# Branch ends of a two-block network: a new order for the two tiles' norms, turns and splits

## The reference, cut to what matters

```python
for layer in range(4):
    g = norm_g[layer]
    h = h + 0.5 * rmsnorm(swiglu(rmsnorm(h, g[0]), ffn_w_in[layer, 0], ffn_w_out[layer, 0]), g[1])
    u = rmsnorm(h, g[2])
    m = mixer(u)          # swa, gla, rwkv7, swa
    h = h + rmsnorm(m, g[3])
    h = h + 0.5 * rmsnorm(swiglu(rmsnorm(h, g[4]), ffn_w_in[layer, 1], ffn_w_out[layer, 1]), g[5])
```

## Time and profile before

| | |
|---|---|
| Median of 3 runs | 3441.63 us (3441.36 to 3445.28) |
| Span of the profiled execution (its own time) | 3441.5 us |
| Instructions in the profile | 49232 |
| TensorE busy | 3274.3 us |
| VectorE busy | 1961.2 us |
| ScalarE busy | 1516.9 us |
| Mean granted TensorE clock | 0.980 |

### The profile page before, as it was taken

The page is one execution under the profiler, slowest core; times in us unless marked ns, Lnnn a source line. Parts: engine busy times, 40 slices in busy tenths (PEclk is TensorE's granted clock), DMA queues, the critical chain, the costliest instruction groups (busy, mean ns, idle before and its releaser), DMA issues.

```text
span 3441.5 us, 49232 instructions
## 1 busy us (share of the span) xinstructions
PE 3274.3 (95%) x21142; PEld 2885.6 (84%) x21142; DVE 1961.2 (57%) x2964; ACT 1516.9 (44%) x2538; POOL 177.4 (5%) x201
## 2 busy tenths in 40 slices
PE   6998999989999999998999999999999999999898
PEld 6987998978898997686989987987878887887797
DVE  4556555557555555674555566555446555825777
ACT  3445444454444443213444454444544434524554
POOL 0000000003000000140000000001001000100100
PEclk9999999999999999998999999999999999999999
DMA  6563656555556544414556554551013333531452
GB/s 225 184 201 105 208 184 210 188 177 178 190 184 210 189 154 154 142 44 137 187 191 208 184 176 153 184 179 28 26 62 110 110 121 136 173 97 62 134 185 98
DMA packets 411238, 521.99 MB, mean 152 GB/s; under 512 B 41575, under 2 KB 353500, under 8 KB 410892
## 3 DMA queue, kind: packets, MB, share of 16 engines
q1 hardware_dynamic: 405980, 516.23, 45.7%
q0 software_dynamic: 816, 2.10, 0.2%
q10 hardware_dynamic: 4224, 0.52, 0.1%
HBM read 516.19 MB, written 2.10 MB: 151 GB/s over the span
## 4 chain that ended last, share of the span: by engine, by line
PE 87%; DVE 7%; ACT 4%; issue 1%; DMA 1%; POOL 0%; SPq 0%; DVEq 0%; ACTq 0%; POOLq 0%
PE ps L186 24%; PE ps L187 24%; PE ps L188 23%; PE ps L178 5%; PE ps L196 3%; PE ps L1226 2%; PE ps L559 1%; PE ps L1938 1%; PE ps L3802 1%; PE ps L3799 1%; DVE small L1283 1%; ACT a L1246 1%; DVE a L716 0%; PE ps L3478 0%; DVE xt L699 0%
## 5 line engine op out<-in xcount | busy, mean ns | idle before, releaser
L186 PE MATMUL ps<-a 128*128 128x256 f32 (+1 forms) x4832 | 1528.4, 316 | 35.5 <-DVE a L716 13.9
L188 PE MATMUL ps<-a 128*128 128x256 f32 (+1 forms) x4664 | 1466.6, 314 | 0.0
L187 PE MATMUL ps<-a 128*128 128x256 f32 (+1 forms) x4536 | 1432.1, 316 | 0.0
L186 PEld LDWEIGHTS ps<-a 128*128 128x128 f32 x4832 | 929.7, 192 | 101.5 <-DVE a L716 13.9
L188 PEld LDWEIGHTS ps<-a 128*128 128x128 f32 x4664 | 897.7, 192 | 52.8
L187 PEld LDWEIGHTS ps<-a 128*128 128x128 f32 x4536 | 873.4, 193 | 50.6
L892 DVE TENSOR_TENSOR a<-ring,a 128x1024 fp32r<-128x1024 f32 x594 | 693.6, 1221 | 350.3 <-ACT a L886 350.3
L886 ACT ACTIVATE a<-ring 128x1024 fp32r<-128x1024 f32 x594 | 585.7, 1047 | 234.6 <-PE ps L188 233.7
L990 ACT ACTIVATE tmp<-ps 128x256 f32<-128x256 f32 x176 | 67.6, 384 | 508.6 <-PE ps L188 508.6
L996 DVE TENSOR_TENSOR a<-tmp,ps 128x256 f32<-128x256 f32 x176 | 74.1, 421 | 300.9 <-ACT tmp L990 300.9
L617 POOL TENSOR_TENSOR small<-small,cst 128x1 f32<-128x1 f32 (+1 forms) x78 | 58.3, 749 | 2806.2 <-DVE small L612 1965.7
(11 more groups left out here) (379 smaller groups left out, 3862.1 us busy)
## 6 DMA issues: line engine op xcount, KB each, us to landing
ring<-in_ffn_w_in_dram SPq DMA_DIRECT2D x220, 1024.0 KB, 7.4
ring<-in_ffn_w_out_dram SPq DMA_DIRECT2D x121, 1024.0 KB, 5.0
ring<-in_ada_w_dram SPq DMA_DIRECT2D x48, 1024.0 KB, 5.4
ring<-in_swa_w_qkv_dram SPq DMA_DIRECT2D x12, 1024.0 KB, 7.9
ring<-in_gla_w_in_dram SPq DMA_DIRECT2D x12, 1024.0 KB, 6.8
ring<-in_rwkv_w_rkv_dram SPq DMA_DIRECT2D x12, 1024.0 KB, 5.1
ring<-in_na_w_qkv_dram SPq DMA_DIRECT2D x12, 1024.0 KB, 5.2
ring<-in_swa_w_o_dram SPq DMA_DIRECT2D x8, 1024.0 KB, 5.7
```

The lines of the kernel that those rows point to most:

```text
L186: pe.x.matmul(out, lh, rh, start=start and i == 0, stop=False)
L187: pe.x.matmul(out, lh, rl, start=False, stop=False)
L188: ins = pe.x.matmul(out, ll, rh, start=False, stop=stop and i == n - 1)
```

## The change

`act_finish`, `dve_finish` and `pe_finish`, which served both kinds of end through flags, are replaced by one function for each kind and engine.

In a feed-forward end VectorE adds tile 0 into h before it splits the opened weights, not after; takes the mean of tile 1 between the two halves of tile 0's gain; scales tile 1 before it splits tile 0; and does both ada pairs at the end. ScalarE squares h of tile 1 before the first ada copy and scales tile 1 before the second. TensorE does the second pair's products into bank 6 instead of bank 3, behind a wait for tile 1's gain product.

In a mixer end TensorE transposes tile 0 inside tile 1's projection, ahead of its last two quarters (the last `k0` step, or `q == 2` of the second half). VectorE takes tile 0's gain between the two scales of tile 1, and its two splits around tile 1's add; the ada pair comes last. ScalarE splits tile 0 before it squares h of tile 1, and copies the ada row after that.

SP's list is the same, and GpSimd's four powers come in the same order.

```diff
--- before.py
+++ after.py
@@ -282,11 +282,14 @@
             load_block(K, sp, (tag, "wo", i, k0), w, k0, 4, i * 512, 512, (K.s.pe, (tag, "wo", tiles[-1], i, k0)))
 
 
-def pe_out(K, pe, tag, x, tiles, first):
+def pe_out(K, pe, tag, x, tiles, first, amid=None):
+
     for t in tiles:
         for i in range(2):
             bank = K.ps[:, 2 * (t + first) + i, :]
             for k0 in (0, 4):
+                if amid is not None and (t, i, k0) == (tiles[-1], 1, 4):
+                    amid()
                 c = K.w[tag, "wo", i, k0]
                 pe.wait_ge(*c.landed)
                 wv = v3(c.buf, 512)
@@ -425,13 +428,16 @@
     sp_splitB(K, sp, S, 0, w, 0, D, lambda i, k0: (K.s.pe, (tag, "wo", tiles[-1], i, k0)))
 
 
-def pe_split_out(K, pe, S, tag, xs, tiles, first, halves=(0, 1)):
+def pe_split_out(K, pe, S, tag, xs, tiles, first, halves=(0, 1), amid=None):
+
     s, (xh, xl) = K.s, xs
     for t in tiles:
         pe.wait_ge(*s.dve.at(tag, "turned", t, 1))
         for i in halves:
             bank = K.ps[:, 2 * (t + first) + i, :]
             for q in range(4):
+                if amid is not None and (t, i, q) == (tiles[-1], 1, 2):
+                    amid()
                 c, raw, wh, wl = S.of(K, 4 * i + q, 512)
                 pe.wait_ge(*s.dve.at("lo", S.tag, 4 * i + q))
                 ins = mm3(pe, bank, [((xh[:, 2 * q + k, tk(t)], xl[:, 2 * q + k, tk(t)]), (wh[:, k, :], wl[:, k, :])) for k in range(2)],
@@ -691,9 +697,9 @@
               ).then_inc(*s.pe.up(tag, t, "turn", half))
 
 
-def dve_gain(K, dve, tag, t, gcol):
+def dve_gain(K, dve, tag, t, gcol, halves=(0, 1)):
     s = K.s
-    for half in range(2):
+    for half in halves:
         f = slice(4 * half, 4 * half + 4)
         dve.wait_ge(*s.pe.at(tag, t, "turn", half))
         dve.x.tensor_tensor(K.xt3(T)[:, f, tk(t)], v3(K.ps[:, 2 * t + half, :], 128), bc(gcol[:, f], 2, [128, 4, 128]),
@@ -708,9 +714,9 @@
         act.x.activation(xh[:, k, tk(t)], K.xt3(T)[:, k, tk(t)], AF.Copy).then_inc(*s.act.up("xh", f, t, half))
 
 
-def dve_split_x(K, dve, f, t):
+def dve_split_x(K, dve, f, t, halves=(0, 1)):
     (xh, xl), s = K.xs[f], K.s
-    for half in range(2):
+    for half in halves:
         k = slice(4 * half, 4 * half + 4)
         dve.wait_ge(*s.act.at("xh", f, t, half))
         dve.x.tensor_tensor(xl[:, k, tk(t)], K.xt3(T)[:, k, tk(t)], xh[:, k, tk(t)].bitcast(F32), SUB).then_inc(
@@ -721,95 +727,113 @@
     return [K.s.dve.at(tag, t, "xt", half) for half in range(2)]
 
 
-def act_finish(K, act, tag, src, ready, nxt, f=None, early=False, pairs=0):
-
+def act_ffn_end(K, act, tag, src, ready, f):
 
     act_square(K, act, tag, 0, src[0], ready[0])
-    if nxt:
-        act_square_h(K, act, tag, 0)
-        if early:
-            act_norm(K, act, tag, 0)
+    act_square_h(K, act, tag, 0)
     act_square(K, act, tag, 1, src[1], ready[1])
-    if nxt and not early:
-        act_norm(K, act, tag, 0)
-    if pairs:
-        act_ada(K, act, 2, 2)
-    if nxt:
-        act_square_h(K, act, tag, 1)
-        if f is not None:
-            act_split_x(K, act, f, 0, xt_ready(K, tag, 0))
-    if pairs == 2:
-        act_ada(K, act, 2, 2)
-    if nxt:
-        act_norm(K, act, tag, 1)
+    act_norm(K, act, tag, 0)
+    act_square_h(K, act, tag, 1)
+    act_ada(K, act, 2, 2)
+    if f is not None:
+        act_split_x(K, act, f, 0, xt_ready(K, tag, 0))
+    act_norm(K, act, tag, 1)
+    act_ada(K, act, 2, 2)
     if f is not None:
         act_split_x(K, act, f, 1, xt_ready(K, tag, 1))
 
 
-def dve_finish(K, dve, tag, src, coef, gcol, f=None, early=False, pairs=0, bias=None, opened=None):
-
-    row, nxt = K.rows[tag, "g"], gcol is not None
+def dve_ffn_end(K, dve, tag, src, gcol, f, opened):
+
+    row = K.rows[tag, "g"]
     for half in range(2):
-        dve_scale(K, dve, tag, 0, half, src[0], row, coef, bias)
-    if opened is not None:
-        dve_open(K, dve, opened, 1)
+        dve_scale(K, dve, tag, 0, half, src[0], row, 0.5)
     dve_add(K, dve, tag, 0)
-    if nxt:
-        dve_mean_h(K, dve, tag, 0)
-        if early:
-            dve_norm(K, dve, tag, 0)
-    dve_scale(K, dve, tag, 1, 0, src[1], row, coef, bias)
-    if nxt and not early:
-        dve_norm(K, dve, tag, 0)
-    dve_scale(K, dve, tag, 1, 1, src[1], row, coef, bias)
+    dve_open(K, dve, opened, 1)
+    dve_mean_h(K, dve, tag, 0)
+    dve_scale(K, dve, tag, 1, 0, src[1], row, 0.5)
+    dve_norm(K, dve, tag, 0)
+    dve_scale(K, dve, tag, 1, 1, src[1], row, 0.5)
     dve_add(K, dve, tag, 1)
-    if nxt:
-        dve_gain(K, dve, tag, 0, gcol)
-    if pairs:
-        dve_ada(K, dve, 2)
-    if nxt:
-        dve_mean_h(K, dve, tag, 1)
-        if f is not None:
-            dve_split_x(K, dve, f, 0)
-        dve_norm(K, dve, tag, 1)
-        dve_gain(K, dve, tag, 1, gcol)
+    dve_gain(K, dve, tag, 0, gcol, (0,))
+    dve_mean_h(K, dve, tag, 1)
+    dve_gain(K, dve, tag, 0, gcol, (1,))
+    dve_norm(K, dve, tag, 1)
+    if f is not None:
+        dve_split_x(K, dve, f, 0)
+    dve_gain(K, dve, tag, 1, gcol)
     if f is not None:
         dve_split_x(K, dve, f, 1)
-    if pairs == 2:
+    for _ in range(2):
         dve_ada(K, dve, 2)
 
 
+def act_mixer_finish(K, act, tag, src, ready, f):
+
+    act_square(K, act, tag, 0, src[0], ready[0])
+    act_square_h(K, act, tag, 0)
+    act_norm(K, act, tag, 0)
+    act_square(K, act, tag, 1, src[1], ready[1])
+    act_split_x(K, act, f, 0, xt_ready(K, tag, 0))
+    act_square_h(K, act, tag, 1)
+    act_ada(K, act, 2, 2)
+    act_norm(K, act, tag, 1)
+    act_split_x(K, act, f, 1, xt_ready(K, tag, 1))
+
+
+def dve_mixer_finish(K, dve, tag, src, gcol, f, bias):
+
+    row = K.rows[tag, "g"]
+    for half in range(2):
+        dve_scale(K, dve, tag, 0, half, src[0], row, 1.0, bias)
+    dve_add(K, dve, tag, 0)
+    dve_mean_h(K, dve, tag, 0)
+    dve_norm(K, dve, tag, 0)
+    dve_scale(K, dve, tag, 1, 0, src[1], row, 1.0, bias)
+    dve_gain(K, dve, tag, 0, gcol)
+    dve_scale(K, dve, tag, 1, 1, src[1], row, 1.0, bias)
+    dve_split_x(K, dve, f, 0, (0,))
+    dve_add(K, dve, tag, 1)
+    dve_split_x(K, dve, f, 0, (1,))
+    dve_mean_h(K, dve, tag, 1)
+    dve_norm(K, dve, tag, 1)
+    dve_gain(K, dve, tag, 1, gcol)
+    dve_split_x(K, dve, f, 1)
+    dve_ada(K, dve, 2)
+
+
 def pool_finish(K, pool, tag, nxt):
-    pool_rsqrt(K, pool, (tag, 0, "y"), K.sm[tag, 0][:, 2:3])
-    if nxt:
-        pool_rsqrt(K, pool, (tag, 0, "h"), K.sm[tag, 0][:, 5:6])
-    pool_rsqrt(K, pool, (tag, 1, "y"), K.sm[tag, 1][:, 2:3])
-    if nxt:
-        pool_rsqrt(K, pool, (tag, 1, "h"), K.sm[tag, 1][:, 5:6])
-
-
-def pe_finish(K, pe, tag, nxt, pairs=0):
-
+    for t in range(2):
+        pool_rsqrt(K, pool, (tag, t, "y"), K.sm[tag, t][:, 2:3])
+        if nxt:
+            pool_rsqrt(K, pool, (tag, t, "h"), K.sm[tag, t][:, 5:6])
+
+
+def pe_ffn_end(K, pe, tag):
 
     s = K.s
-    if pairs:
-        K.free.clear()
-        rows, sums = Turns(K, (2, 3)), Turns(K, (4, 5))
-        pe_ada_products(K, pe, rows)
-    if nxt:
-        pe_turn_norm(K, pe, tag, 0)
-    if pairs:
-        if pairs == 2:
-            m = pe.ada
-            pe.ada += 2
-            pe_ada_products(K, pe, rows)
-            pe.ada = m
-        pe.wait_ge(*s.dve.at(tag, 0, "g1"))
-        pe_ada_turns(K, pe, sums, 2)
-    if nxt:
-        pe_turn_norm(K, pe, tag, 1)
-    if pairs == 2:
-        pe_ada_turns(K, pe, sums, 2)
+    K.free.clear()
+    rows, sums = Turns(K, (2, 6)), Turns(K, (4, 5))
+    pe_ada_products(K, pe, rows)
+    pe_turn_norm(K, pe, tag, 0)
+    m = pe.ada
+    pe.ada += 2
+    pe.wait_ge(*s.dve.at(tag, 1, "g1"))
+    pe_ada_products(K, pe, rows)
+    pe.ada = m
+    pe.wait_ge(*s.dve.at(tag, 0, "g1"))
+    pe_ada_turns(K, pe, sums, 2)
+    pe_turn_norm(K, pe, tag, 1)
+    pe_ada_turns(K, pe, sums, 2)
+
+
+def pe_mixer_finish(K, pe, tag):
+
+    K.free.clear()
+    pe_ada_products(K, pe, Turns(K, (2, 3)))
+    pe.wait_ge(*K.s.dve.at(tag, 0, "g1"))
+    pe_ada_turns(K, pe, Turns(K, (4, 5)), 2)
+    pe_turn_norm(K, pe, tag, 1)
 
 
 
@@ -1031,7 +1055,7 @@
         if f == 0:
             pe_first(K, pe)
     pe_core(K, pe, f)
-    pe_finish(K, pe, ("f", f), K.ffn[f].gcol is not None, 2)
+    pe_ffn_end(K, pe, ("f", f))
     K.s.pe.seal("end", ("f", f))
 
 
@@ -1045,7 +1069,7 @@
             act_split_x(K, act, f, t, xt_ready(K, K.ffn[f].normed, t))
     act_core(K, act, f, act_silu)
     act_open(K, act, f)
-    act_finish(K, act, ("f", f), down_banks(K), down_halves(K, f), K.ffn[f].gcol is not None, K.ffn[f].next, False, 2)
+    act_ffn_end(K, act, ("f", f), down_banks(K), down_halves(K, f), K.ffn[f].next)
     K.s.act.seal("end", ("f", f))
 
 
@@ -1082,7 +1106,7 @@
             dve_split_x(K, dve, f, t)
     dve_core(K, dve, f, dve_gate)
     dve_open(K, dve, f, 0)
-    dve_finish(K, dve, ("f", f), down_banks(K), 0.5, K.ffn[f].gcol, K.ffn[f].next, False, 2, None, f)
+    dve_ffn_end(K, dve, ("f", f), down_banks(K), K.ffn[f].gcol, K.ffn[f].next, f)
```

(16 more changed lines are left out.)

## The result

The changed kernel takes 3429.72 us (median of 4 runs, 3428.72 to 3430.52); the kernel before took 3443.45 us on the same chip (4 runs, 3441.36 to 3445.46). The ratio is 0.9958, with a 95% interval from 0.9944 to 0.9972: about 14 us, or 0.4%, faster. The profiled run took 3430.12 us, with a span of 3428.1 us.

What follows compares the result with a forecast made beforehand. TensorE, busy 95% of the span, bounds the kernel; only its gaps and half clock can be won. 3441.5 - 11.5 (feed-forward ends) + 0.6 (mixer ends) - 3.0 (clock) = 3427.6, stated as 3427.5 us, range 3420 to 3436.5.

Steps and rivals of the forecast that it cites:

- step 1: Feed-forward end, VectorE: tile 0's add no longer waits for the opened weights' split, so it starts about 0.96 us earlier.
- step 2: Feed-forward end, VectorE: tile 1's mean follows its squares with only half the gain ahead, winning another 0.79 us.
- Step 3: Feed-forward end, GpSimd: the power takes 0.55 us instead of 0.93 beside a neighbour reading PSUM; 0.38 won.
- Step 4: Feed-forward end: VectorE's norm of tile 1 starts 2.19 us earlier, at 229.70; ScalarE's half at 230.21, turn halves 230.25, 231.0.
- Step 5: Feed-forward end, VectorE: tile 0's split now stands between tile 1's norm and gain, leaving 2.0 us of the 2.19.
- Step 6: Feed-forward end, TensorE queue: the ada rows' turn ends before tile 1's turn can start, delaying nobody, 0.4 us to spare.
- Step 7: Feed-forward ends before a mixer: both ada pairs come last on VectorE, TensorE begins at 235.1; 1.7 us won, f4 0.4.
- SP: Transfers: SP's list is untouched, slots are freed about 1 us earlier in f0's end, and no transfer is on this chain.
- Clock: TensorE's half-clock stretches after the ends: shorter gaps win back 3.0 us, bounds 0 and 8.4; f3's 2.3 should return.
- The wait moves on: Rival, feed-forward ends: only the 0.96 earlier add holds, the queue behind eats the rest; 3436.3 us, chance 0.18.
- Clock back almost everywhere: Rival: the same steps, with the half-clock loss of 8.4 us won back whole; 3422.2 us, chance 0.16.
- Slower: Rival: TensorE idles in one longer piece, seven ends each bring a 3.05 us half-clock stretch; 3452 us, chance 0.05.

Runs made afterwards that it cites:

- the fillers' profile: Changed kernel plus unread 256-column TensorE products in its gaps, behind mixer ends' ada products and last turns and ending f0, f2, f4, f6; 3415.21 us, ratio 0.9925.
- the old mixer ends and fillers: Changed feed-forward ends with the previous kernel's mixer ends, plus unread 256-column products in TensorE's gaps; 3420.43 us, ratio 0.9935 to the kernel before.
- the mixer ends alone: Mixer ends as changed, feed-forward ends as in the kernel before; 3438.0 us, ratio 0.9987 to the kernel before.
- the kernel with the late split: Changed kernel, but mixer ends split tile 0's first half after tile 1's add, second half after its norm; 3431.11 us, ratio 0.9964 to the kernel before.

## Why the prediction was right, step by step

The forecast was 3427.5 us within 3420 and 3436.5, and 3429.72 was measured. The sum was made on spans, and there it came to 3427.6 against 3428.1. A run's time is not its span, though: in the changed kernel's profiled run it is 2.0 us longer, while the prediction took the two for equal within 0.1. So of the 2.2 us by which the time missed, most is that mix-up and little the mechanism.

- **Steps 1 to 3.** The add at 221.51 (predicted 221.46), the mean at 228.73 (228.69), the power 0.55. Undoing step 1 costs 0.93 to 0.98 (priced at 0.96), undoing step 2 0.8 (0.79). Step 3's cause is shown; its 0.38 on the chain can be read only from the starts in the timeline.
- **Step 4.** VectorE's norm at 229.74 (229.70), ScalarE's at 230.25 (230.21), the turn's halves at 230.28 and 231.01 (230.25, 231.0). One sign of being wrong was ill chosen: ScalarE's half is the last by 0.73 us (done at 230.96 against 230.23), more than the 0.5 named, but by the prediction's own sum it had to be, and it holds nobody, since VectorE takes the gain only at 231.35.
- **Step 5.** The gain at 231.35, as predicted, and the split of tile 1 at 232.73 (232.75). f1, f3, f5 won 1.93 on average (2.0), but the parts are 2.28, 1.76 and 1.74. The 2.0 was read from f0, and in the kernel before f0's turn of tile 1 ran partly at half clock; f5's did not:

```profile
232.43 1.72 PE L196 MATMUL ps<-cst,hc 128*128 128x128 f32 x8 [2.34 <-DVE hc L677]
...
1807.30 1.09 PE L196 MATMUL ps<-cst,hc 128*128 128x128 f32 x8 [2.34 <-DVE hc L677]
```

  From VectorE's norm to its split of tile 1 it took 2.90 us in f0, 3.15 in f1 and 2.61 in f3 and f5. So the new order is worth 1.75 a time, and the other 0.25 of the 2.0 was clock. That the three together came out near 6.0 is luck: f1's old end had 0.54 of it.
- **Step 6.** The ada turn ran at 229.24 to 229.90, 0.38 ahead of tile 1's turn: nobody waited for it.
- **Step 7.** TensorE began at 234.88, 0.2 sooner than predicted: the two ada pairs took 0.69 together, not 0.8. f0, f2, f6 won 1.78 on average (1.7), f4 0.49 (0.4). This average mixes too: 2.01, 1.25 and 2.07. f0 and f6 had half clock in their old turns, worth 0.29 and 0.54; f2 and f6 were held up after the change (f2 as the last section tells, f6 by what follows here).
- **SP.** "No transfer is on this chain" holds for f0, not for f6, so this term should not have been nothing there. There ScalarE's split of the mixer's weights waits for a load, and the squares behind it start late, 0.4 us in the kernel before and 0.6 after:

```profile
1980.41 2.01 ACT L352 ACTIVATE a<-ring 128x1024 fp32r<-128x1024 f32 x2 [0.47 <-DMA ring<-in_swa_w_qkv_dram]
```

- **Mixer ends.** +0.2 in gla and rwkv (+0.3), -0.1 in swa0 and +0.2 in swa1 (0). The transposes cost 0.88 (0.93), the half split 0.40 (0.43).
- **Clock.** The sum, 2.3 us between the ends against 3.0, was near; the parts were not. f3's stretch returned its 2.4 as predicted, and f1, f3, f5 are followed by 1.00. But the loss from f2 to gla rose from 1.39 to 4.13, that behind f4 from 1.58 to 2.92 and that from f6 to swa1 from 3.41 to 4.82; f0's stretch was gone and an equal one stood in swa0's attention (3.09 before, 3.41 after). Gla to f3 gained 1.5, rwkv to f5 1.5 and what follows swa1 2.8, where no gain was foreseen. This term came out right by opposite misses: luck.
- **The rivals.** *The wait moves on* is out: undoing steps 1 and 2 brings each one's price back whole wherever nothing else held the end up. *Clock back almost everywhere* is out, though the fillers' profile (19.7 us of half-clock loss less) shows that more than its 8.4 us was there to be won. *Slower* is out, but something like its mechanism is there behind three ends: TensorE began gla at 0.50 for 5.9 us (2.8 before), rwkv for 5.8 (3.2 before) and swa1 for 2.8 (none before). That cost 1.3 to 1.4 us more at each, not 3.05, and decided nothing, as the 3.3 us of half-clock loss inside the ends of f0, f2 and f6 are gone.

## What to carry to other kernels

Follow one repeated end through all engines, price each move by its own row, and multiply: at nearly full TensorE use, seven ends that won 0.5 to 2.3 us each made 11.6 of the 13.4 us. Take the price from an end without a half-clock stretch, or the clock is counted as order. When a wait's line shrinks, look which line has taken its place in the queue before you count it. Where the granted clock drops behind gaps that can't be closed, a few idle products, cut to fit the gap, gave nearly as much again (11 us by the ratios) as the reordering of three engines (14 us); measure one before choosing how many.

## What the runs showed that was not expected

- **A plain fp32 product costs nearly four times a split one.** A filler with 512 columns left two records and took 0.89 us (4.46 for five), one with 256 columns 0.46. The matmuls of `mm3`, on operands split into a high and a low part, leave one record and start every 0.23 us at 512 columns, so one filler takes nearly four times as long. The kernel before showed it already: an ada pair is 16 matmuls in `pe_ada_products` and 32 records in the trace, which is why it passes for 32 products.
- **The clock's stretches wander.** Nearly the same instructions between two ends (the eight transposes come or go) lost 0 to 15.3 us to half clock (f0 to swa0: 3.1 before, 3.4 after, 0 with the short fillers, and 15.3 with the old mixer ends and fillers). Their changes, more than any edit of 0.5 us, go with the spread of the runs: 14.5 us for the mixer ends alone.
- **A late start without a reason in the trace.** In f2's end of the changed kernel the add starts 0.43 us after the power has ended, on a free VectorE:

```profile
727.49 0.55 POOL L623 TENSOR_TENSOR small<-small,cst 128x1 f32<-128x1 f32 x1 [189.48 <-DVE small L618]
...
728.47 1.42 DVE L661 SCALAR_TENSOR_TENSOR h<-tmp,small,h 128x512 f32<-128x512 f32 x2 [0.46 <-POOL small L623]
```

  f0's add follows after 0.08 (220.88 + 0.55 to 221.51). It is most of why f2 won 1.25 and not 1.7, and why f2 lost only 0.60 when the split went back ahead of the add: the split hides it. It is no chance of one run. Of the eleven profiled kernels that add first, nine show 0.42 or 0.43 here; the two with one VectorE instruction more in each end (beside the power) show 0.07. What it is stays open.

  f6 is another case. Its add follows the power at once (0.09), but in the changed kernel all of tile 0 is 0.6 us late there, by the load that ScalarE waits for (above): its end is 12.29 us, and 11.70 in the kernel with the late split, where that load did not hold ScalarE. With the split ahead of the add it did not either, so the 0.33 that f6 lost there is the price less this 0.6.
